# A trunk layer on one core: the adaLN opening with weights in another order, two of its pieces on TensorE and the modulation on ScalarE

## The reference, cut to what matters

```python
c_act = jax.nn.silu(c)
mod = (c_act @ w_ada[i] + b_ada[i])[:, None, :]
sh1, sc1, g1, sh2, sc2, g2 = jnp.split(mod, 6, axis=-1)
h = rms_norm(x) * (1 + sc1) + sh1
proj = h @ w_in[i]
# ... RG-LRU, RWKV-7 and sliding-window attention branches from proj,
# ... gated sum, output projection, SwiGLU feed-forward part
```

## Time and profile before

| | us |
|---|---|
| median of 3 runs | 2896.04 |
| lowest and highest run | 2893.48 and 2904.6 |
| the profiled execution, its own time | 2904.03 |
| the profiled execution, its span | 2902.2 |
| TensorE busy | 2824.1 (97%) |
| VectorE busy | 1465.3 (50%) |
| ScalarE busy | 765.1 (26%) |
| GpSimd busy | 775.6 (27%) |

### The profile page before, as it was taken

The page is one execution under the profiler, slowest core; times in us unless marked ns, Lnnn a source line. Parts: engine busy times, 40 slices in busy tenths (PEclk is TensorE's granted clock), DMA queues, the critical chain, the costliest instruction groups (busy, mean ns, idle before and its releaser), DMA issues.

```text
span 2902.2 us, 60941 instructions
## 1 busy us (share of the span) xinstructions
PE 2824.1 (97%) x25827; PEld 2361.5 (81%) x25827; DVE 1465.3 (50%) x1579; ACT 765.1 (26%) x1107; POOL 775.6 (27%) x510
## 2 busy tenths in 40 slices
PE   4999999999999999999999999999999999999999
PEld 3798979898888888877877777888888888888887
DVE  5745555545464646487774666566654222222223
ACT  4312121313131312145455777011122000000001
POOL 0403030403030312134341112333333333333332
PEclk9999999999999999999999999999999999999999
DMA  5201020202020101133322112465311111111112
GB/s 195 75 28 59 20 64 15 75 4 76 11 69 24 56 25 45 41 126 112 119 81 55 57 45 76 157 209 190 104 44 58 51 43 51 51 45 49 51 46 77
DMA packets 222623, 201.54 MB, mean 69 GB/s; under 512 B 22369, under 2 KB 193467, under 8 KB 222395
## 3 DMA queue, kind: packets, MB, share of 16 engines
q1 hardware_dynamic: 208928, 150.70, 17.2%
q10 hardware_dynamic: 13467, 47.31, 4.6%
HBM read 167.57 MB, written 30.41 MB: 68 GB/s over the span
## 4 chain that ended last, share of the span: by engine, by line
PE 90%; DVE 4%; ACT 3%; issue 2%; DMA 1%; SPq 0%; POOL 0%; ACTq 0%; DVEq 0%; POOLq 0%
PE ps L255 66%; PE ps L891 3%; PE ps L905 3%; PE ps L902 2%; PE ps L869 2%; PE ps L954 1%; PE ps L1091 1%; PE ps L859 1%; PE ps L1116 1%; PE ps L1104 1%; DVE arena L1987 1%; DMA arena<-in_w_ada 1%; PE ps L825 1%; PE ps L911 1%; PE ps L938 1%
## 5 line engine op out<-in xcount | busy, mean ns | idle before, releaser
L255 PE MATMUL ps<-x_hi,w_hi 128*128 128x512 f32 (+1 forms) x2544 | 820.1, 397 | 4.0 <-POOL w_lo L247 1.3
L255 PE MATMUL ps<-x_lo,w_hi 128*128 128x512 f32 (+1 forms) x2544 | 803.9, 391 | 0.0
L255 PE MATMUL ps<-x_hi,w_lo 128*128 128x512 f32 (+1 forms) x2544 | 803.1, 391 | 0.0
L245 POOL CAST w_hi<-w_raw 128x1024 fp32r<-128x1024 f32 (+2 forms) x221 | 211.7, 958 | 1999.5 <-PE ps L255 1596.2
L255 PEld LDWEIGHTS ps<-x_hi,w_hi 128*128 128x128 f32 (+1 forms) x2544 | 471.4, 188 | 119.4 <-issue 20.0
L255 PEld LDWEIGHTS ps<-x_hi,w_lo 128*128 128x128 f32 (+1 forms) x2544 | 478.5, 188 | 103.3
L255 PEld LDWEIGHTS ps<-x_lo,w_hi 128*128 128x128 f32 (+1 forms) x2544 | 478.6, 188 | 99.5
L247 POOL TENSOR_TENSOR w_lo<-w_raw,w_hi 128x1024 fp32r<-128x1024 f32 (+2 forms) x221 | 483.2, 2187 | 17.7
L255 PE MATMUL ps<-hid,w_hi 128*128 128x512 f32 (+1 forms) x928 | 256.5, 395 | 3.8 <-DVE mod L2007 3.0
L2283 DVE TENSOR_TENSOR arena<-ps,arena 128x1024 f32<-128x1024 f32 x21 | 25.7, 1225 | 373.8 <-PE ps L255 373.8
L255 PEld LDWEIGHTS ps<-hid,w_hi 128*128 128x128 f32 (+1 forms) x928 | 170.8, 188 | 46.8 <-issue 13.9
(11 more groups left out here) (289 smaller groups left out, 3443.3 us busy)
## 6 DMA issues: line engine op xcount, KB each, us to landing
w_raw<-in_w_in SPq DMA_DIRECT2D x78, 512.0 KB, 4.0
arena<-in_w_ada SPq DMA_DIRECT2D x48, 512.0 KB, 5.8
w_raw<-in_w_ffn_in SPq DMA_DIRECT2D x44, 512.0 KB, 3.8
arena<-gates_sig ACTq DMA_DIRECT2D x40, 512.0 KB, 4.2
gates_sig<-arena ACTq DMA_DIRECT2D x24, 512.0 KB, 2.6
w_raw<-in_w_ffn_out SPq DMA_DIRECT2D x22, 512.0 KB, 3.6
arena<-in_x SPq DMA_DIRECT2D x16, 512.0 KB, 7.0
y_a<-arena ACTq DMA_DIRECT2D x10, 512.0 KB, 2.6
```

What stands on the lines that cost most here:

```text
L245: nc.gpsimd.tensor_copy(hi, raw).then_inc(s_whi, 1)
L255: ins = nc.tensor.matmul(dst[h], wp, xp[h], start=first and m == 0, stop=last and m == 2)
```

## The change

The shift and scale columns of w_ada are now cut by k tiles of the output rather than into shift and scale: pieces 0 to 7 hold, for the eight blocks of 128 rows, the 512 shift columns and the 512 scale columns of k tiles 0 to 3; pieces 8 to 15 hold those of k tiles 4 to 7. A piece still has 512 KB, in two runs of 2 KB a row rather than one of 4 KB. The parts under one semaphore are smaller. Pieces 8 and 9 are not multiplied on VectorE: TensorE takes them directly, as matmuls of 128 by 128 weights against a column of silu(c) (line 788 of the kernel after), eight columns for each. The reciprocal stands behind two pieces rather than five. The modulated tile is made by ScalarE from PSUM (line 1374 after) just ahead of the high part of the same k tile. The sums of the second half are taken by TensorE within the loop over the k tiles, at k = 2, and the transposes of k tile 4 move between the two lora blocks there. All accumulation within a half now goes to one accumulator, so that each product step waits for the one just before it.

```diff
--- before.py
+++ after.py
@@ -200,16 +200,25 @@
         p0_pe, p0_act, p0_dve = made_by("pe", "start_pe"), made_by("act", "start_act"), made_by("dve", "start_dve")
         ada_out, ada_pe = made_by("dve", "mod_columns_ready"), made_by("pe", "mod_columns_done")
         ADA0, ADA_SLOTS = 2 * KT, 12
-        ADA_ACC0, ADA_OUT0 = ADA0, 3
-        ADA_PARTS = [(0, 5), (5, 9), (9, 13), (13, 15), (15, 16)]
+        ADA_ON_PE = (8, 9)
+        ADA_ACC0, ADA_OUT0 = ADA0 - len(ADA_ON_PE), 2 + len(ADA_ON_PE)
+        ADA_PARTS = [(0, 2), (2, 5), (5, 8), (8, 10), (10, 12), (12, 14), (14, 16)]
         s_ada = [sem(f"ada_weights_loaded_{k}") for k in range(len(ADA_PARTS))]
-        ADA_COLS = [(0, 8), (8, 10), (10, 16)]
+        def ada_part(n):
+            return next((k, n1 - n0) for k, (n0, n1) in enumerate(ADA_PARTS) if n0 <= n < n1)
+        def mod_half(half):
+            return mod[:, 0:2 * KT].rearrange("p (o k) -> p o k", o=2)[:, :, half * KT // 2:(half + 1) * KT // 2]
         ada_acc = made_by("dve", "ada_products_summed")
         s_mod = sem("modulation_inputs_loaded")
         ada_fix = made_by("dve", "mod_scales_ready")
-        h_pe, h_tmp, h_hi, h_lo = made_by("pe", "xnT_done"), made_by("dve", "h_ready"), made_by("act", "h_high"), made_by("dve", "h_low")
+        h_pe, h_tmp, h_hi, h_lo = made_by("pe", "xnT_done"), made_by("act", "h_ready"), made_by("act", "h_high"), made_by("dve", "h_low")
         passed = {"SP": sem("sp_waits_passed"), "Pool": sem("pool_waits_passed"), "DVE": sem("dve_waits_passed"),
                   "PE": sem("pe_waits_passed")}
@@ -540,8 +549,9 @@
                 for n in range(n0, n1):
                     if n >= ADA_SLOTS:
                         sp.wait_ge(ada_acc, upto(n - ADA_SLOTS + 1))
-                    src = w_ada[n // 2 * P:(n // 2 + 1) * P, n % 2 * 1024:(n % 2 + 1) * 1024]
-                    sp.dma_start(ada_w0[:, n % ADA_SLOTS, :], src).then_inc(s_ada[part], 16)
+                    half, row = n // KT, n % KT
+                    src = w_ada[row * P:(row + 1) * P, 0:2048].rearrange("p (o n) -> p o n", o=2)[:, :, half * 512:(half + 1) * 512]
+                    sp.dma_start(halves(ada_w0[:, n % ADA_SLOTS, :]), src).then_inc(s_ada[part], 16)
             load_block(sp, Block("lora", 2), cols(w_in, COL_LORA + 2 * P, 32), 32)
             load_gains(sp)
@@ -760,27 +770,41 @@
                     ins = pe.transpose(ps[:, 4 + 2 * (k % 2) + t // 4, (t % 4) * P:(t % 4 + 1) * P], xs[:, t, k * P:(k + 1) * P], ident)
                 ins.then_inc(h_pe, 1)
+            def mod_sums(half, bank):
+                pe.wait_ge(ada_acc, upto(KT if half == 0 else ADA_ACC0))
+                for c in range(KT):
+                    ins = mm(ps[:, bank, c:c + 1], ada_acc0[:, half, c * P:(c + 1) * P], ones[:, 0:1], start=True, stop=True)
+                ins.then_inc(ada_pe, 1)
+            mod_sums(0, 0)
             pe.wait_ge(p0_act, upto(18))
             for k in range(2):
                 transpose_x(k)
-            for part, (c0, c1) in enumerate(ADA_COLS):
-                half = c0 // 8
-                pe.wait_ge(ada_acc, upto(ADA0 - 1 + half))
-                for c in range(c0, c1):
-                    ins = mm(ps[:, part, c:c + 1], ada_acc0[:, half, c % 8 * P:(c % 8 + 1) * P], ones[:, 0:1], start=True, stop=True)
+            for q, n in enumerate(ADA_ON_PE):
+                part, count = ada_part(n)
+                pe.wait_ge(s_ada[part], 16 * count)
+                for c in range(KT):
+                    ins = mm(ps[:, 1 + q, c:c + 1], ada_w0[:, n % ADA_SLOTS, c * P:(c + 1) * P], mod[:, 48 + n % KT:49 + n % KT], start=True, stop=True)
                 ins.then_inc(ada_pe, 1)
             lora = [Block("lora", c) for c in range(2)]
             for blk in lora:
                 pe.wait_ge(s_wsplit, upto(blk.before + 1))
-            pe.wait_ge(ada_out, upto(3))
+            pe.wait_ge(ada_out, upto(1 + len(ADA_ON_PE)))
             for k in range(KT):
                 if k + 2 < KT:
                     pe.wait_ge(h_tmp, upto(k + 1))
-                    transpose_x(k + 2)
+                    if k == 2:
+                        mod_sums(1, 4)
+                    else:
+                        transpose_x(k + 2)
                 pe.wait_ge(h_lo, upto(k + 1))
                 for blk in lora:
+                    if k == 2 and blk is lora[1]:
+                        pe.wait_ge(ada_out, upto(ADA_OUT0))
+                        transpose_x(k + 2)
                     w = [t[:, blk.slot, k * P:(k + 1) * P] for t in (w_hi, w_lo)]
                     x = [[t[:, k, h * 512:(h + 1) * 512] for h in range(2)] for t in (x_hi, x_lo)]
                     ins = three_passes([ps[:, 2 * blk.slot + h, :] for h in range(2)], w, x, k == 0, k == KT - 1)
@@ -1343,6 +1367,11 @@
             act.wait_ge(lam_s, upto(2))
             fn(rate2, rate, ACT.Exp, scale=-1.0).then_inc(p0_act, 1)
             for k in range(KT):
+                act.wait_ge(h_pe, upto(k + 1))
+                act.wait_ge(ada_out, upto(1 if k < KT // 2 else ADA_OUT0))
+                if k >= 2:
+                    act.wait_ge(h_lo, upto(k - 1))
+                fn(halves(h_tmpb[:, k % 2, :]), pair_of(2 + k % 2), ACT.Identity, scale=mod[:, MOD_SC1 + k:MOD_SC1 + k + 1], bias=mod[:, MOD_SH1 + k:MOD_SH1 + k + 1]).then_inc(h_tmp, 1)
                 act.wait_ge(h_tmp, upto(k + 1))
                 fn(x_hi[:, k, :], h_tmpb[:, k % 2, :], ACT.Copy).then_inc(h_hi, 1)
@@ -1748,46 +1777,55 @@
             dve.wait_ge(lam_s, upto(2))
             dve.wait_ge(p0_act, upto(1))
-            for part, (n0, n1) in enumerate(ADA_PARTS):
-                for n in range(n0, n1):
-                    c_k, acc = mod[:, 48 + n // 2:49 + n // 2], ada_acc0[:, n % 2, :]
-                    if n == n0:
-                        dve.wait_ge(s_ada[part], 16 * (n1 - n0))
-                    if n < 2:
-                        ins = v.tensor_scalar(acc, ada_w0[:, n % ADA_SLOTS, :], c_k, None, ALU.mult)
-                    else:
-                        dve.wait_ge(ada_acc, upto(n - 1))
-                        ins = v.scalar_tensor_tensor(acc, ada_w0[:, n % ADA_SLOTS, :], c_k, acc, ALU.mult, ALU.add)
-                    ins.then_inc(ada_acc, 1)
-                if part == 0:
-                    dve.wait_ge(p0_act, upto(10))
-                    step(v.reciprocal(rstd, rstd))
-            def ada_add(part):
-                c0, c1 = ADA_COLS[part]
-                dve.wait_ge(ada_pe, upto(part + 1))
-                v.tensor_tensor(mod[:, c0:c1], ps[:, part, c0:c1], mod[:, c0:c1], ALU.add).then_inc(ada_out, 1)
-            ada_add(0)
-            ada_add(1)
-            dve.wait_ge(ada_out, upto(2))
-            def modulate(k):
-                dve.wait_ge(h_pe, upto(k + 1))
-                if k >= 2:
-                    dve.wait_ge(h_lo, upto(k - 1))
-                v.tensor_scalar(halves(h_tmpb[:, k % 2, :]), pair_of(2 + k % 2), mod[:, MOD_SC1 + k:MOD_SC1 + k + 1], mod[:, MOD_SH1 + k:MOD_SH1 + k + 1],
-                                ALU.mult, ALU.add).then_inc(h_tmp, 1)
-            modulate(0)
-            ada_add(2)
-            for k in range(KT):
-                if k + 1 < KT:
-                    if k == 1:
-                        dve.wait_ge(ada_out, upto(3))
-                    modulate(k + 1)
+            def ada_piece(n):
+                c_k, acc, first = mod[:, 48 + n % KT:49 + n % KT], ada_acc0[:, n // KT, :], (0, KT + len(ADA_ON_PE))
+                done = n if n < KT else n - len(ADA_ON_PE)
+                part, count = ada_part(n)
+                dve.wait_ge(s_ada[part], 16 * count)
+                if n in first:
+                    ins = v.tensor_scalar(acc, ada_w0[:, n % ADA_SLOTS, :], c_k, None, ALU.mult)
+                else:
+                    dve.wait_ge(ada_acc, upto(done))
+                    ins = v.scalar_tensor_tensor(acc, ada_w0[:, n % ADA_SLOTS, :], c_k, acc, ALU.mult, ALU.add)
+                ins.then_inc(ada_acc, 1)
+            added = [0]
+            def ada_add(half, bank):
+                dve.wait_ge(ada_pe, upto(added[0] + 1))
+                if half == 1:
+                    dve.wait_ge(ada_out, upto(added[0]))
+                v.tensor_tensor(mod_half(half), ps[:, bank, 0:KT].rearrange("p (o k) -> p o k", o=2), mod_half(half), ALU.add).then_inc(ada_out, 1)
+                added[0] += 1
+            def h_low(k):
                 dve.wait_ge(h_hi, upto(k + 1))
                 v.tensor_tensor(x_lo[:, k, :], h_tmpb[:, k % 2, :], x_hi[:, k, :].bitcast(F32), ALU.subtract).then_inc(h_lo, 1)
+            ada_piece(0)
+            ada_piece(1)
+            dve.wait_ge(p0_act, upto(10))
+            step(v.reciprocal(rstd, rstd))
+            for n in range(2, KT):
+                ada_piece(n)
+            ada_add(0, 0)
+            ada_piece(10)
+            for q in range(len(ADA_ON_PE)):
+                ada_add(1, 1 + q)
+            ada_piece(11)
+            h_low(0)
```

(9 more changed lines are left out.)

## The result

Over seven runs of each, the kernel after takes 2915.79 us (2909.59 to 2918.9) against 2896.56 us of the kernel before (2893.48 to 2904.6). The ratio is 1.0055, with a 95% interval of 1.0046 to 1.0065: **slower by half a per cent**, some 16 us by the ratio; the two medians stand 19.2 us apart. The forecast was 2894.3 and no change that can be told; the time lies well outside its range.

What follows compares the result with a forecast made beforehand. TensorE, busy 97% of the span, was taken as the bound, with gains only where it stands still in the opening. Terms -3.7 + 2.2 - 0.2 = -1.7 us on the 2896.04 median gave 2894.3, range 2889.5 to 2900.0.

Steps and rivals of the forecast that it cites:

- Steps 1 to 5: Path from reciprocal through the k-tile loop: dense matmuls 3.7 us earlier, 2.2 us back for sums, 0.2 us wait gone.
- The column sums: TensorE's first-half sums, ahead of the transposes: eight columns, half of the 16 that took 4.37 us, so 2.2 us.
- the direct pieces: Pieces 8 and 9 on TensorE after the 16 transposes: 16 columns, 4.37 us, ending at 44.0.
- The sums at k = 2: Second-half column sums inside the k-tile loop: 2.2 us added there, with 1.7 us as the lower bound.
- the first dense k tile: k = 0 of the dense matmul loop, starting at 46.8: taken as 4.28 us.
- Step 6: DMA queue and everything past the opening: same DMAs, mask load and next weights about 2 us earlier, no cost.
- The clock in the loop over the k tiles: Rival: sums within dense work lower the granted clock, 3.4 us more, 2897.7 us; chance 0.12.
- The clock is up earlier: Rival: unbroken opening work raises TensorE's clock, k = 0 takes 2.77 us, 1.5 us more gained, 2892.8; chance 0.10.
- The 2 KB rows: Rival: w_ada pieces with 2 KB rows land slower, piece 7's product 3.1 us late, 2897.4 us; chance 0.08.
- taken up behind it: Rival: something after 78.6 us absorbs the opening's gain and the end stays at 2896.0 us; chance 0.10.
- slower by over 0.5%: Outcome class for the whole kernel: a loss past half a per cent, 14.5 us; chance 0.02.

Runs made afterwards that it cites:

- e1: Kernel before with 65 empty semaphore increments on TensorE ahead of the first transposes of x: 2923.52 us, ratio 1.0076.
- e5: Kernel after with 191 further TensorE instructions (empty increments and unused single-column matmuls) spread over stretches where TensorE waits: 2902.37 us, ratio 0.9996.
- e2: Kernel after with 191 empty semaphore increments on TensorE ahead of the first transposes: 2913.18 us, ratio 1.0044.
- e4: Kernel before with 32 empty semaphore increments on TensorE ahead of the first transposes: 2898.17 us in one run.
- e12: Kernel before with 50 empty increments, 25 at each of two places where TensorE waits anyway: 2912.16 us in one run.
- e9: Kernel after with pieces 8 and 9 back on VectorE and the later products reordered around the low parts: 2894.53 us, ratio 0.9975.
- e11: Kernel after with the modulated tile made on VectorE again, the first two while it waits for TensorE: 2934.41 us in one run.
- e10: Kernel after with the reciprocal put back behind five products: 2923.77 us in one run.

## Why the prediction was wrong

**Steps 1 to 5, the opening: right in mechanism but for the clock, half in size.** The reciprocal ran at 24.81 (forecast 25.44), the first half's products ended at 33.98 (33.9), VectorE stood in front of the adds until 44.65 (44.0), dense matmuls started at 47.21 (46.8). These terms were off. Products that wait for the one just before start 1.39 us apart (25.73, 27.13, 28.51 in the chain), not 1.31. The column sums took 3.58 rather than 2.2, and the direct pieces 3.52 rather than 4.37, both from one row of before, 4.37 for 32 records, which hid two paces: 0.11 us a record until 46.4, 0.21 behind. In the kernel after it is 0.21 a record until 40.9 and 0.11 from 41.1, so the sums went at the slow pace and the pieces at the fast one. The sums at k = 2 took 1.68, the lower bound, rather than 2.2. And the first dense k tile took 4.89 rather than 4.28: the clock was back at 51.3, 4.1 us behind the first dense matmul, against 2.7 before. Dense matmuls started 3.25 us earlier, 0.61 went into that tile and 1.68 into the sums: 0.9 gained, 1.7 forecast.

**Step 6 failed**, in its last sentence: "Counters past the opening only begin at other numbers." I asked of the instructions behind the opening what they wait for, and of those ahead only how long they take. I did not ask where they lie. The step put at nothing what moving the loop's code does. The added instructions cost 65 places, and with these places the kernel is 16 us slower than before, the loop 14.3 us in the profiled executions. e1 shows it with the change left out (ratio 1.0076), e5 with the change left in (0.9996 once the code lies 256 places on).

The Trainium skill has the rule, in "Runtime: NRT & Kernel Launch", Instruction fetch mechanics: TensorE's instruction memory is refilled in blocks of 16 KiB, 256 instructions, and fetched ahead in sequence; a taken branch to a place that is not held makes it wait for a fetch. The trace agrees with the size (16.4 KB a packet) and with the place of the stall: a turn of 4510 records is longer than the 2048 instructions that the page gives for TensorE's memory, and only turns that are entered by the jump stall; the feed-forward turn of 594 is shorter, and no packet starts there. That a shift of 256 restores the loop (e2, e5) agrees with 256 a block. The page also says that crossing a block's end is mostly hidden; behind the jump of the kernel after it is not, and whether it is in the middle of a turn is open.

How I read the head, from e1, e4, e12 and the kernels: the jump fetches the block of its target, and what is left of that block must last until the next one is there. With a shift of 65 it holds up to the 15th or so of a turn's matmul instructions, 1.6 us of work, and TensorE runs dry; with 50 it holds 15 more, dense ones, and nothing is lost. The traces, in which each packet has its own time, bear this out. In all fourteen, a packet of instructions starts within 1 us of the start of each turn from the second on; so the fetch is not what the shift adds. In the four kernels at a shift of 65 the late matmul follows that packet: in the 28 turns the packet ends 0.98 to 1.86 us into the turn and the late weight load starts 2.33 to 3.26 us into it, always 1.19 to 1.61 us behind the packet's end (mean 1.38), and where the packet ends later the load starts later (correlation 0.87). In turn 3 of the kernel after the packet runs from 383.71 to 384.99, and the matmul comes at 386.36. What fills the 1.4 us between packet and load no run shows.

**The rivals.** The clock in the loop over the k tiles did not fall behind the sums of the kernel after. It stood at 0.50 from 44.6 to 51.2, as before from 46.5 to 53, by the stretches after (columns as rows 6), and by the trace it stayed at 1.00 from there through the sums at 55.74 to the end of the RWKV loop:

```profile
41.10:44.40 3.30, 3.30 (x33) 3.30 (x31) 0.17 (x1) 2.79 (x3) 0.00 (x0) 1.00 0.00 0
44.60:51.20 6.60, 5.95 (x18) 4.71 (x18) 6.44 (x7) 2.26 (x2) 0.00 (x0) 0.50 0.01 2
51.40:55.00 3.60, 3.60 (x22) 3.04 (x21) 3.09 (x3) 1.96 (x2) 0.00 (x0) 1.00 0.00 0
```

The mechanism is real all the same: in e9, behind a wait of 1.04 us and the sums, and in e11, behind a gap of 0.2 us and the sums, the clock was at 0.50 for 3.4 us. It had 0.12 of the chances.

"The clock is up earlier" came half true. Its condition did: the pace rose at 41.1, after 7 us of work without a gap. But TensorE then waited from 44.5 to 45.1 for VectorE's add and the clock was at 0.50 by 44.6, so dense work gained nothing; in e9, without that wait, k = 0 took 2.86 us, about the 2.77 that this rival had named. The rows were misread against it: before, too, the pace went from 0.21 to 0.11 us a record, at 43.5, so that the slow level did not hold through the opening.

The 2 KB rows cost nothing that can be seen: pieces 2 to 4 were there at 25.66, against 25.90 before. The gain of the opening was not taken up behind it, it was paid back with 13 us more, by something that none of the rivals named. Without it the time would have lain in the range: e5's ratio of 0.9996 makes 2895.4 of the kernel before's 2896.56 (an estimate). The chances went wrong there too: "slower by over 0.5%" had 0.02, since only mechanisms of the opening were weighed, and none of these could reach 14.5 us. For a kernel whose loops run eight times behind the edit, a loss outside the edit's own stretch needed a chance of its own.

**What stays open.** The middle of a turn, where TensorE issues 64x64 matmuls as fast as it gets them, loses 0.9 us at a shift of 65, 1.2 at 50 and 0.6 to 0.8 at 130. Its waits lie at several lines (915, 929, 952 after) and not in every turn, and they add up to 2.6 us of the 6.5; the wait at line 964 lies behind the middle, and before has its like at line 938. That the middle follows the shift is shown by the four kernels at 65 (79.82 to 81.27) against the four at 0, 1 and 256 (78.81 to 79.06), one profiled execution each; 50 rests on one, 130 on two. Which boundary meets which jump or wait was not settled. e10 and e11, with the same shift, lose 0.4 and 1.4 us more there; the other engines' fetches may take part, and this was not tried. Why the clock falls for longer in some executions than in others, which moves single runs by up to 6 us, is not known either. And no shift other than those in the table was run, so that the loss repeats every 256 instructions rests on 256 and 288 alone.

## What to carry to other kernels

When an edit adds or takes away instructions ahead of a long loop, its cost is not only their time: count them on that engine, and expect the loop to move against its fetch blocks; here that was worth half a per cent. Before judging an edit of a few us, run it once more with empty instructions in idle places that bring the loop back to its old place (256 in all, or zero). And an engine that is queued in front of another's result, as VectorE was for six us, can cost more than the work that was taken from it: with the two pieces given back, dense matmuls started 3.7 us sooner than in the kernel after, and the kernel was 7 us faster than before, 3.6 of them by the start of the RWKV loop.

## What the runs showed of the hardware

- An empty semaphore increment takes 0.15 us on TensorE: 191 of them delayed the sums of e2 by 12.4 us, behind an idle stretch of some 16.
- A stall of up to 1.0 us ahead of one matmul, 1.4 in the first 200 instructions of a turn, in each turn after the first, depends on 15 instructions more or less of code ahead (after and e1 at a shift of 65 against e12 at 50). The late weight load starts 1.19 to 1.61 us behind the end of a 16 KB packet of instructions, in 28 turns of four kernels.
- A loop of 4510 TensorE records a turn draws 20 such packets in each turn (19 at a shift of 130), a loop of 594 none.
- The stretch between the two loops takes 1026.7 to 1033.0 us in fourteen executions, and goes with 6.8 to 20.4 us in it at a granted clock of 0.50.
- A float32 product on VectorE of 128x1024 takes 1.28 us; a chain of them starts every 1.39 us if each waits for the one before, and every 1.22 if for the one before the last.
- The granted clock of the kernel after reads 1.00 ahead of 41 us, while its transposes and single columns go at 0.22 us a record until then and at 0.11 from 41.1 (32 records in 3.52). The pace tells the level there, the column does not.
